# Two products behind each norm run their high parts first, the third norm's factor is put on behind the products, and the bias table is written during the FFN

## What is computed

```python
def first_block(x, c, ...):
    sh1, sc1, g1, sh2, sc2, g2 = jnp.split(jax.nn.silu(c) @ w_ada + b_ada, 6, axis=-1)
    x = x + g1 * hybrid_mixer(modulate(rms_norm(x, norm1_w), sh1, sc1), ...)
    x = x + g2 * swiglu(modulate(rms_norm(x, norm2_w), sh2, sc2), w_ffn_in, w_ffn_out)
    shf, scf = jnp.split(c_act @ w_ada_f + b_ada_f, 2, axis=-1)
    return modulate(rms_norm(x, normf_w), shf, scf)

def second_block(x, ...):              # its x is the first block's output
    q, k, v = split(rms_norm_2(x, attn_norm) @ w_qkv)
    s = q @ k.T * Dh ** -0.5 + rel_bias[bucket(q_pos - k_pos)]   # causal, 16 heads
    x = x + (softmax(s) @ v) @ w_o
    x = x + conv_ffn(rms_norm_2(x, ffn_norm), w_up, conv_w, conv_b, w_down)
    return rms_norm_2(x, final_norm)
```

## Time and profile before

| | before |
|---|---|
| median of 3 runs | 971.01 us (970.1 to 972.38) |
| profiled execution | 971.41 us, of which 969.6 us are its span |
| TensorE matmul busy | 923.2 us, 95% of the span |
| VectorE, ScalarE, GpSimd busy | 69%, 52%, 7% of the span |
| mean granted TensorE clock | 0.987 of full speed |

### The profile page before, as it was taken

The page is one execution under the profiler, slowest core; times in us unless marked ns, Lnnn a source line. Parts: engine busy times, 40 slices in busy tenths (PEclk is TensorE's granted clock), DMA queues, the critical chain, the costliest instruction groups (busy, mean ns, idle before and its releaser), DMA issues.

```text
span 969.6 us, 18556 instructions
## 1 busy us (share of the span) xinstructions
PE 923.2 (95%) x7996; PEld 879.0 (91%) x7996; DVE 667.0 (69%) x1113; ACT 505.1 (52%) x821; POOL 65.8 (7%) x91
## 2 busy tenths in 40 slices
PE   5789999999999999999999998989999999999997
PEld 2588888898899999989999998979998999999997
DVE  3877677557579986778777845465656677777643
ACT  2576666544344565465444433456566566565442
POOL 0101011011000000030000001010000300000001
PEclk9789999999999999999999999999999999999999
DMA  8733222232259975446777879514332355545631
GB/s 332 281 146 114 88 92 99 81 123 89 89 174 359 355 285 218 174 175 260 264 266 270 295 198 248 207 62 183 131 134 97 119 191 195 180 174 170 233 120 44
DMA packets 27681, 177.31 MB, mean 183 GB/s; under 512 B 2864, under 2 KB 5680, under 8 KB 7504
## 3 DMA queue, kind: packets, MB, share of 16 engines
q1 hardware_dynamic: 27600, 176.13, 51.2%
HBM read 174.29 MB, written 1.84 MB: 182 GB/s over the span
## 4 chain that ended last, share of the span: by engine, by line
PE 81%; DVE 7%; ACT 7%; DMA 4%; issue 1%; SPq 0%; DVEq 0%; ACTq 0%
PE ps L1002 45%; PE ps L1008 22%; DMA raw<-in_w_fo_dram 3%; PE ps L1000 2%; ACT wh L1343 1%; DVE tmp L1658 1%; PE ps L1046 1%; DVE wl L1696 1%; PE ps L1054 1%; PE ps L1140 1%; PE ps L1201 1%; PE ps L1006 1%; PE ps L1157 1%; DMA raw<-in_ada_dram 1%; PE ps L1057 1%
## 5 line engine op out<-in xcount | busy, mean ns | idle before, releaser
L1696 DVE TENSOR_TENSOR wl<-raw,wh 128x1024 fp32r<-128x1024 f32 x265 | 321.5, 1233 | 100.4 <-ACT wh L1343 100.0
L1002 PE MATMUL ps<-HH,wh 128*128 128x256 f32 x1480 | 387.0, 293 | 3.0 <-DVE wl L1696 2.1
L1002 PE MATMUL ps<-HH,wl 128*128 128x256 f32 x1480 | 374.7, 285 | 0.0
L1343 ACT ACTIVATE wh<-raw 128x1024 fp32r<-128x1024 f32 x265 | 273.0, 1041 | 160.7 <-PE ps L1008 91.6
L1002 PEld LDWEIGHTS ps<-HH,wh 128*128 128x128 f32 x1480 | 286.4, 194 | 11.3 <-issue 4.2
L1002 PEld LDWEIGHTS ps<-HH,wl 128*128 128x128 f32 x1480 | 286.7, 194 | 1.9 <-issue 1.9
L1008 PE MATMUL ps<-HL,wh 128*128 128x256 f32 x1480 | 240.6, 285 | 2.6 <-DVE HL L1671 2.2
L1008 PEld LDWEIGHTS ps<-HL,wh 128*128 128x128 f32 x1480 | 206.5, 194 | 3.3 <-DVE HL L1671 2.6
L1002 PE MATMUL ps<-FH,wh 128*128 128x256 f32 x352 | 89.4, 283 | 3.7 <-DVE wl L1696 3.7
L1002 PE MATMUL ps<-FH,wl 128*128 128x256 f32 x352 | 89.6, 285 | 0.0
L1631 DVE SCALAR_TENSOR_TENSOR acc<-raw,silc,acc 128x512 f32<-128x512 f32 x101 | 76.6, 759 | 8.6 <-DMA raw<-in_ada_dram 5.4
(11 more groups left out here) (251 smaller groups left out, 1084.8 us busy)
## 6 DMA issues: line engine op xcount, KB each, us to landing
raw<-in_ada_dram SPq DMA_DIRECT2D x32, 1024.0 KB, 5.2
raw<-in_w_fi_dram SPq DMA_DIRECT2D x22, 1024.0 KB, 4.8
raw<-in_w_up_dram SPq DMA_DIRECT2D x22, 1024.0 KB, 4.8
raw<-in_w_rest_dram SPq DMA_DIRECT2D x20, 1024.0 KB, 4.8
raw<-in_w_in_dram SPq DMA_DIRECT2D x16, 1024.0 KB, 4.8
raw<-in_w_qkv_dram SPq DMA_DIRECT2D x12, 1024.0 KB, 4.8
raw<-in_w_o_dram SPq DMA_DIRECT2D x8, 1024.0 KB, 4.8
raw<-in_w_fo_dram SPq DMA_DIRECT2D x8, 1024.0 KB, 9.6
```

What stands on the lines that cost most here:

```text
L1002: e.matmul(o, w[:, k, 128 * t:128 * t + 128], x_hi[:, k0 + k, :], start=first and n + k == 0, **MM)
L1343: e.activation(whl[u % HALF][0][:, 0:n], raw[i % RAW][:, c:c + n], ACT.Copy).then_inc(*a_hi.up(u))
L1696: e.tensor_tensor(wl[:, 0:n], raw[i % RAW][:, c:c + n], wh[:, 0:n].bitcast(F32), ALU.subtract).then_inc(*v_lo.up(u))
```

## The change

1. **High parts first.** The first two products behind N1, N3 and N4 (`fg 0` and `fu 0`, `q2 0` and `k2 0`, `ug 0` and `uv 0`) run as one (`high_first`): all their matmuls with `HH`, 64 of them, then all with `HL`, 32. Accordingly `apply` writes all scaled tiles and high parts first, then all low parts, and the low parts are all on VectorE.
2. **Weights ahead.** Before `close`, `low_of` asks for the low splits of the next four units; the small vectors of the modulation are computed before `close` too.
3. **N3's factor behind the products.** At N2 the high part is made directly, `(X*R)*w1n + shn` with `w1n = (1+scale)*normf*attn_norm` and `shn = shift*attn_norm` (ScalarE); the stream (`stream`, VectorE) and its squares follow. N3's factor `R3` is made after `k2 0` (`third_scale`: one sum matmul, ScalarE's Ln and Exp), and multiplied to the products when they leave PSUM: q with `R3/8` (the attention's scale) and k with `R3` on VectorE (`normed`), v with a column of it on ScalarE. Attention heads begin two ticks after `k2`.
4. **Table early.** `bias` stands after `fg 2`, the load of `DC` ahead of `fg 1`, the write to scratch ahead of `fg 4`. The loads of `U` stay ahead of the third `fo`.

```diff
     def apply(n):
         for j in range(4):
             scale(n, j)
-            if j:
-                parts(n, j - 1)
-        parts(n, 3)
+            emit("high", n, j, held[j])
+        for j in range(4):
+            if n == N3:
+                emit("stream", j, held[j])
+            emit("low", n, j, held[j])
+            tmp.give(held[j], v_norm, "lo", n, 2 * j + 1)
+            if n == N3:
+                s, before = sq.take()
+                emit("sq", N3, j, s, before, part[0] if j else None)
+                if j:
+                    sq.give(part[0], g_norm, "part", N3, j)
+                part[:] = [s]
+    def third_scale():
+        misc.order[:] = [b for b in misc.order if b[0] == 3]
+        bank, before = misc.take()
+        emit("norm_sum", N3, part[0], bank, before)
+        sq.give(part[0], p_norm, "sum", N3)
+        emit("norm_r", N3, bank)
+        made.add("norm_r3")
+        misc.give(bank, a_norm, "ln", N3)
+        for _ in range(4):
+            yield
+        bank, before = yield from take(misc)
+        emit("norm_col", N3, bank, before)
+        made.add("norm_col")
+        misc.give(bank, a_norm, "col")
+    def scaled_out(p):
+        kind, j, bank = p["kind"], p["j"], p["banks"][0]
+        while ("norm_col" if kind == "v2" else "norm_r3") not in made:
+            yield
+        if kind == "v2":
+            emit("plain", p["p"], 0)
+            main.give(bank, a_ev, "plain", p["p"])
+        else:
+            emit("normed", p["p"], 0)
+            main.give(bank, v_ev, "normed", p["p"])
+        made.add((kind, j))
+        if kind == "k2":
...
+            if j == 2:
+                bank, before = misc.take()
+                emit("bias", 0, 0, bank, before)
+                misc.give(bank, v_misc, "rb")
             while not tmp.order:
...
                 misc.give(4, v_att, "lo", dict(open_heads)[0])
...
-            for t in range(2):
-                main.give(banks[t], v_ev, "x", n, 6 + t)
             if n == N1:
                 mod(4)
                 mod(3)
                 emit("mod_scale", n, 0)
-                apply(n)
             elif n == N2:
                 mod(7)
                 mod(6)
                 emit("mod_scale", n, 0)
-                bank, before = misc.take()
-                for i in range(4):
-                    emit("shift", n, i)
-                    if i:
-                        s, sfree = sq.take()
-                        emit("norm_sq", N3, i - 1, s, sfree, bank, before if i == 1 else None)
-                        sq.give(s, p_norm, "sq", N3, i - 1)
-                s, sfree = sq.take()
-                emit("norm_sq", N3, 3, s, sfree, bank, None)
-                sq.give(s, p_norm, "sq", N3, 3)
-                wbank, wfree = misc.take()
-                emit("norm_r", N3, bank, wbank, wfree)
-                misc.give(wbank, p_norm, "warm", N3)
-                misc.give(bank, a_norm, "ln", N3)
-                apply(N3)
-                misc.order[:] = [b for b in misc.order if b[0] == 3]
-            elif n == N4:
-                apply(n)
+            if n != N5:
+                low_of(p["units"][-1] + HALF - 1)
+            close(n, p)
+            for t in range(2):
+                main.give(banks[t], v_ev, "x", n, 6 + t)
+            if n == N5:
+                emit("finish")
             else:
-                emit("finish")
...
             return [("oa", 2 * kt + n) for kt in kts for n in range(2)]
...
+    def high_first(ps):
+        last = ps[0]["units"][0] + HALF - 1
+        for p in ps:
+            for n in range(2):
+                run_unit(p, n, last, "high")
+        for p in ps:
+            for n in range(2):
+                split_up_to(p["units"][n] + HALF - 1)
+                run_unit(p, n, None, "low")
+            close_product(p)
...
...
-            if i == named["fo", 0]["items"][0]:
+            if i == named["fg", 1]["items"][0]:
                 v_ev.wait_ge(e, "value", "m", 3)
                 e.dma_start(DC[:, :], a["dist"]).then_inc(*d_dc.up("dc"))
-            if i == named["fo", 1]["items"][0]:
+            if i == named["fg", 4]["items"][0]:
...
-        if first:
+        if first and part != "low":
             free(e, p["free"][b])
         v_lo.wait_ge(e, u)
-        for k in range(kn):
+        for k in range(kn) if part != "low" else ():
             high_of(e, src, k0 + k)
             for n, w in enumerate((wh, wl)):
...
                 else:
                     e.matmul(o, w[:, k, 128 * t:128 * t + 128], x_hi[:, k0 + k, :], start=first and n + k == 0, **MM)
-        for k in range(kn):
...
-        ins.then_inc(*p_mm.up(u, t))
+        if part != "high":
+            ins.then_inc(*p_mm.up(u, t))
...
-            elif kind == "norm_r" and ev[1] == N3:
-                warm(e, N3, *ev[3:])
+            elif kind == "norm_col":
+                b = ev[2]
+                free(e, ev[3])
+                a_norm.wait_ge(e, "r", N3)
+                for t in range(2):
+                    ins = e.matmul(psum[b][:, t:t + 1], R3[0:1, cs[t]], ones[0:1, 0:1], start=True, **MM)
+                ins.then_inc(*p_norm.up("col"))
+            elif kind == "norm_sum":
+                _, n, s, b, before = ev
+                free(e, before)
+                g_norm.wait_ge(e, "part", n, 3)
+                e.matmul(psum[b][:, 0:T], ones, sqs[s][:, 0:T], start=True, **MM).then_inc(*p_norm.up("sum", n))
             elif kind == "close":
...
+            a_norm.wait_ge(e, "col")
+            e.activation(VA[:, 0, 256 * j:256 * j + 256], bank[:, 0:T], ACT.Copy, scale=r3c[:, 0:1]).then_inc(
+                *a_ev.up("plain_0", n))
+            ins = e.activation(VA[:, 1, 256 * j:256 * j + 256], bank[:, T:2 * T], ACT.Copy, scale=r3c[:, 1:2])
         ins.then_inc(*a_ev.up("plain", n))
...
+    def act_high(e, n, j, m):
+        finished(e, named[before_write[n]])
+        for kt in (2 * j, 2 * j + 1):
+            src, dst = tmps[m][:, T * (kt % 2):T * (kt % 2) + T], HH[:, kt, :]
+            v_norm.wait_ge(e, "scaled", n, kt)
+            if n == N1:
+                mod_ready(e, 6, 7)
+                ins = e.activation(dst, src, ACT.Identity, bias=modc[:, 24 + kt:25 + kt])
+            elif n == N3:
+                v_norm.wait_ge(e, "w1n")
+                ins = e.activation(dst, src, ACT.Identity, scale=w1n[:, kt:kt + 1], bias=shn[:, kt:kt + 1])
+            else:
+                ins = e.activation(dst, src, ACT.Copy)
+            ins.then_inc(*a_norm.up("hi", n, kt))
...
-                p_norm.wait_ge(e, "sq", n, 3)
+                p_norm.wait_ge(e, *(("sum", N3) if n == N3 else ("sq", n, 3)))
+                act_ln_exp(e, n, b)
                 if n == N3:
-                    v_norm.wait_ge(e, "shift", 7)
-                act_ln_exp(e, n, b)
+                    a_norm.wait_ge(e, "r", N3)
+                    e.activation(R3q[:, :], R3[:, :], ACT.Copy, scale=0.125).then_inc(*a_norm.up("rq"))
+            elif kind == "norm_col":
+                p_norm.wait_ge(e, "col")
+                e.activation(r3c[:, :], psum[ev[2]][:, 0:2], ACT.Copy).then_inc(*a_norm.up("col"))
             elif kind == "sq":
                 _, n, j, s, before, _ = ev
...
     def dve_scale(e, n, j, m, before):
-        a_norm.wait_ge(e, "r", n)
+        a_norm.wait_ge(e, "r", N2 if n == N3 else n)
         if n in (N0, N1):
             v_norm.wait_ge(e, "w1c", n, j // 2 if n == N0 else 0)
         free(e, before)
+        if n == N3 and j > 1:
+            x_ready(e, N2, 2 * j)
+            x_ready(e, N2, 2 * j + 1)
+            e.tensor_tensor(pair(tmps[m]), X[:, 2 * j:2 * j + 2, :], R[:, None, :].broadcast_to([128, 2, T]),
+                            ALU.mult).then_inc(*v_norm.up("scaled", n, 2 * j + 1))
+            v_norm.at[("scaled", n, 2 * j)] = v_norm.at[("scaled", n, 2 * j + 1)]
+            return
         for kt in (2 * j, 2 * j + 1):
...
-            ins = e.tensor_tensor(HL[:, kt, :], src, high, ALU.subtract)
-        ins.then_inc(*v_norm.up("lo", n, kt))
+        e.scalar_tensor_tensor(out=HL[:, kt, :], in0=tmps[m][:, 0:T], scalar=modc[:, kt:kt + 1],
+                               in1=HH[:, kt, :].bitcast(F32), op0=ALU.add, op1=ALU.subtract).then_inc(
+            *v_norm.up("lo", n, kt))
+    def dve_stream(e, j, m):
+        mod_ready(e, 12, 13)
+        v_norm.wait_ge(e, "w1c", N2, 0)
+        for kt in (2 * j, 2 * j + 1):
+            v_norm.wait_ge(e, "scaled", N3, kt)
...
+    def dve_low(e, n, j, m):
+        for kt in (2 * j, 2 * j + 1):
+            src, high = tmps[m][:, T * (kt % 2):T * (kt % 2) + T], HH[:, kt, :].bitcast(F32)
+            a_norm.wait_ge(e, "hi", n, kt)
+            if n == N1:
+                ins = e.scalar_tensor_tensor(out=HL[:, kt, :], in0=src, scalar=modc[:, 24 + kt:25 + kt], in1=high,
+                                             op0=ALU.add, op1=ALU.subtract)
...
+        if n == N2:
+            mod_ready(e, 12, 13)
```

(39 more changed lines are left out.)

153 lines of the change are left out of this document (74 added, 79 removed).

## The result

The kernel after took 955.79 us in the median of four runs (955.5 to 956.38), the kernel before 970.65 (970.1 to 972.38) beside it: a ratio of 0.985, 95% interval 0.983 to 0.987. The profiled execution's span is 953.8 us, 15.8 less than before; the medians differ by 14.9, because the profiled execution of before was 0.8 us above its median.

The account below looks back on a forecast made before the run. TensorE, busy 923.2 of 969.6 us, was taken as the bound, so only gaps between its matmuls could win. N3 8.7, N1 1.4, N4 1.4 and table 5.4 made 16.9 us: 971.0 to 954.1 us, 8-in-10 range 951.8 to 958.2.

Parts of the forecast that it names:

- N3, 8.7: At N2/N3: second scaling directly behind N2's `R` and the pair ending sooner gain 9.2 us, less 0.5 for contention.
- the extra split: At N2: the low split now ahead of `close` on VectorE delays the second `X` and all behind it by 1.27 us.
- the half clock: At N3: the stretch of 16 matmuls 0.21 us apart would be gone, 1.5 us.
- the sum matmul: Behind N3's pair: one sum matmul follows, between nothing and 0.60 us, taken as 0.4.
- The first tile: In N3's pair: the first output tile needs 1.50 us instead of 0.96, 0.54 lost.
- The 0.5 taken off for contention: At N3: 0.5 us deducted for what VectorE and GpSimd do to each other, bounded at 0 and 3.5.
- N1 and N4, 1.4 each: First 12 matmuls behind N1 and N4 fall from 3.47 and 3.40 us to 1.98; gain 1.4 each.
- The table, 5.4: Early table write: all 5.8 us of `fo` loss go, less 0.1 at the start and 0.3 at `fg 4`.
- rival (a): At `fg 4`: the table write delays its weights for longer, 2 us plus 1.5 of clock, 957.3 us; chance 0.10.
- Behind the pair, nothing: Behind N3's pair: q and k evacuated on VectorE, `R3` ready before the heads ask; net nothing.
- Full pace, 0.12 us a matmul: All products on TensorE: unheld matmuls take 0.12 us each, so a `fo` product of 132 is 15.84 us.
- The sum: Whole kernel: 8.7 + 1.4 + 1.4 + 5.4 = 16.9 us gained, from 971.0 to 954.1 us.

Follow-up runs that it names:

- a_split: Kernel after, with the extra low split at N2 alone put behind `close` instead of ahead of it: 955.27 us, ratio 0.984.
- b_table: Kernel before with only the fourth part of the change, the early table: 966.61 us, ratio 0.9945.
- b_pad64: Kernel before with one unused tile of 64 bytes a partition behind `w1c`, nothing else: 969.69 us, ratio 0.999.
- a_qlate: Kernel after, with q's evacuation on VectorE one tick later, behind the four heads' bias additions: 950.62 us, ratio 0.978.
- b_hh64: Kernel before with one unused tile of 64 bytes ahead of `HH`, nothing else: 962.27 us, ratio 0.989.
- a_serial: Kernel after, with the paired products behind N1, N3 and N4 run one after the other on TensorE: 964.72 us, ratio 0.993.

## Why the prediction was right, and where only in sum

954.1 was forecast, 955.8 came. Point by point:

- **N3, 8.7.** Measured 8.9. The first matmul was put 5.2 us behind the sum's first, and came at 5.4; the extra split cost its 1.27 us (a_split took 1.31 back); the half clock didn't return (but b_table and b_pad64 had none at N3 either, with the old order, so the 1.5 us that the prediction counted for it were partly luck); the sum matmul took 0.25 instead of 0.4. The first tile lost 0.76 instead of 0.54 (629.73 to 631.45 for its eight high matmuls instead of 0.96). The 0.5 taken off for contention was wrong in kind. The contention came and was larger: beside GpSimd two stream operations took 1.58 us instead of 0.73, two low parts 1.91 instead of 0.88. But VectorE was done at 639.2 and TensorE never waited for it, so it cost nothing. The stream operations, with a single SBUF tensor as input, I had called safe by a rule of the Trainium skill (SBUF — State Buffer, Who interferes with whom). It exempts such instructions only outside the two-port modes, and this form looks to be in one (argued from durations, not tested). In the attention the same form took 0.29 us for 128 elements a partition (L1676) and 0.35 for 256 (L1677): 0.06 us for 128 more. The two-input form took 0.36 for 256 (L1751) and 0.64 for 512 (L1743): 0.14 us for 128 more.
- **N1 and N4, 1.4 each.** 1.4 and 1.5.
- **The table, 5.4.** 5.3 by b_table's ratio, with no wait at `fg 4` (0.3 expected): rival (a) didn't occur. In the kernel after ScalarE's split for it ended at 477.7, in time.
- **Behind the pair, nothing.** This step failed, by 4.0 us. It read: "Q and k leave PSUM on VectorE, 8 operations of 0.7 us or less; VectorE is 69% busy overall and their banks are wanted one product later." That answers who waits for the bank, not who stands behind the waiting instruction in VectorE's queue. Behind it stood the additions for four heads, in two rounds (`q2 2` and `q2 3`). The stage lost 4.4 us (4.0, and 0.4 that `wo2`'s pace hid), and a_qlate shows that moving q behind the additions takes 3.9 of them back. The other 0.5 stay open; the half-clock stretch, which after and a_qlate have there and before has not, is large enough for them. The order of VectorE's instructions around `QA`, written down before the run, would have shown it.
- **Full pace, 0.12 us a matmul.** This step failed too, in the other direction. It was read from rows of before and taken as TensorE's limit; after, `fo` and `dn` ran at 0.1175 (61.95 us / 528 = 0.1173 in `fo`), which gave 1.4 us in each and some 0.4 in `wo2`.
- **The sum.** 8.9 + 1.4 + 1.5 + 5.8 (`fo`'s waits) + 1.4 + 1.4 (pace in `fo` and `dn`) - 4.0 (attention, `wo2`'s pace in it) - 0.55 (start) = 15.85 of span. Two misses of opposite sign, about 4.4 down and 3.2 up, nearly cancelled: that the forecast of 16.9 us came so close to the measured 14.9 (15.8 of span) is luck to that extent. With these two left out the measured terms add up to 17.6, less 0.55 at the start.

## What to carry to other kernels

When work moves to another engine, price its place in that engine's queue: an instruction that waits for a product holds up all that stands behind it, and the cure may be one step of order. For matmuls like these, try the stationary and the moving operand 64 bytes apart modulo 128 (32 did as well in most products, but not in all) and compare the distance of successive matmuls, not the busy share: 64 bytes ahead of one tile were worth about 11 us in the kernel before and 10 in the kernel after. A change that only adds a small tile moves all tiles behind it, so look at a stage that the change leaves alone before its gain or loss is put down to the change.

## What the runs showed of the hardware that was not expected

- TensorE has several steady paces at the full granted clock: 12 matmuls of 256 columns in 1.44, 1.41, 1.40 or 1.36 us, set partly by where the input stands against the weights modulo 128 bytes (above).
- The half-clock stretch wanders. With the same order of work it stood behind N3 in before (0.83 from 642 to 652 us), in the attention and behind N4 in b_pad64 (0.57 from 740 to 744, 0.86 from 764 to 774), behind N2 and again behind N3 in b_hh64 (0.57 from 638 to 642 and from 648 to 652), and nowhere at N3 in b_table. So it isn't a property of one gap. At a granted clock of 0.83 over 10 us or 0.57 over 4 some 1.7 us of TensorE's time are lost; in a_serial (0.57 from 634 to 642) it was twice that.
- VectorE and GpSimd slowed each other at N3. A stream operation of VectorE, which has one input tile, took up to 0.83 us instead of 0.40, a low part 1.03 instead of 0.47, and a sum on GpSimd 1.00 instead of 0.74.
